# A routed mixer loop: x is added before the routing work of VectorE, the choice is cut in two, the router's tanh moves by a step

## The chip, the cores and the metric

The kernel runs on one core of a Trainium2 chip. The metric is the device time of one execution in microseconds (us). TensorE multiplies matrices, VectorE, ScalarE and GpSimd work element by element (GpSimd also issues the indirect DMAs), and SyncE issues the plain DMAs. Each engine takes its instructions in program order and waits at semaphores for the others.

## The reference

The kernel computes one layer of a hybrid backbone over 2048 tokens of width 1024. Only the part around the change is shown:

```
x  = x + g1 * mixer(modulate(rmsnorm(x)))      # mixer: LRU half yl, retention half y, times w_out
h2 = modulate(rmsnorm(x))
s  = sigmoid(h2 @ w_router)                    # 64 experts
sb = s + b_router
group score = sum of the two largest sb in each of 8 groups; the best 4 groups stay
eidx  = the 6 largest sb of those groups
gates = s[eidx] / sum(s[eidx]) * 2.5
x  = x + g2 * (routed experts of h2 + shared expert of h2);  out = rmsnorm(x)
```

## The kernel before

The program runs in stages. `front` makes the projections and the LRU. `mixer_out` makes the retention output, the output projection, the residual, the second norm and the routing. `experts` makes the experts, and `final` the last norm. The change is in `mixer_out`, and in the one place of `experts` that routes the last tile.

`mixer_out` is a software pipeline over 16 tiles of 128 tokens (NT = 16). Each engine runs `step(n, par)` for n = -1 to 17, and in step n it works on tiles of different age: `on(n, lag)` guards the work on tile t = n - lag. In program order one step holds:

- **TensorE**: transposes of q for tile n (L1667); the first half of the output products of yl for tile n-1, which waits for the first half of the x of tile n-2 (L1652); transposes of y (L1680); the scores s of tile n, which wait for the tanh of tile n-3 (L1688); `rank` of tile n-4 (L1292); the second half of the yl products and the y products (L1652); transposes of h2 for tile n-2 (L1710); the retention output o of tile n (L1720 to L1722); the router product r of tile n-2 (L1730).
- **VectorE**: qf (L1594), the low part of y (L1598), masked scores (L1601), the low part of yl (L1603); h2 times its norm for tile n-2 (L1609); `place(n-4)`; `choose(n-3)`; the sum x1 of tile n-1 (L1624); y of tile n (L1630).
- **ScalarE**: copy of q (L1539), high part of y (L1543), squares of x1 (L1550), high part of yl (L1554), copies of the transposed h2 (L1560), squares of o (L1567), tanh and sigmoid of the router's product of tile n-2 (L1574, L1576).
- **GpSimd**: qb (L1498) and the retention state (L1500, L1505) of tile n; the norm of tile n-2 (L1512, L1515) and the sum h2 + b2 (L1517); the norm rh of tile n (L1522, L1524); `enlist(n-4)`, which writes the ids (L1313) and issues six indirect DMAs into the experts' lists (L1317).
- **SyncE**: loads of rec, x and yl for tile n+1, of which x and yl wait for the x1 of tile n-1; stores of h2, of its transpose and of x1.

`choose` (L1250) has two halves in one function: 14 counted instructions that find the 6 experts and end in `chosen` (L1277), and then L1278 to L1283, which pick the scores of the 6, sum them, take the reciprocal and write the gates into `entry`. ScalarE's tanh overwrites `th` and then `s`, and so it waits for `entry_done` of the tile before. The router's product and the scores share the PSUM bank `ps_s`.

Of the kernel before, what the change touches and what calls it, by code (L numbers as in the profile page):

```python
# [23 lines left out]
ACT = mybir.ActivationFunctionType  # L24
# [1163 lines left out]
class Routing:  # L1188


    N_TOP = 18

# [57 lines left out]
def choose(dve, R, t, b):  # L1250
# [4 lines left out]
    for g in range(N_GROUPS):  # L1255
# [20 lines left out]
    wait_over_zero(dve, R.rank_done, t)  # L1276
    dve.tensor_reduce(R.chosen[:], R.eq6[:, b].rearrange("p j e -> p e j"), AX.X, ALU.add).then_inc(R.chosen_done, 1)  # L1277
    tops.of(dve.tensor_tensor(R.prod[:], R.eq6[:, b], R.s[:, None, :].broadcast_to(each), ALU.mult))  # L1278
    tops.of(dve.tensor_reduce(R.sel[:], R.prod[:], AX.X, ALU.add))
# [4 lines left out]
                      ALU.mult, ALU.mult).then_inc(R.entry_done, 1)  # L1284
    assert tops.n == R.N_TOP

# [34 lines left out]
def mixer_out(nc, for_dma, io, mod_d, hx_d, rec_d, yl_d, h2_d, h2t_d, sum_d, list_d, sf, ident, R, pre, pre_loaded):  # L1321
# [4 lines left out]
    with ExitStack() as ctx:  # L1326
# [84 lines left out]
        def on(n, lag):  # L1411

            return not isinstance(n, int) or 0 <= n - lag < NT
# [118 lines left out]
        @block.scalar  # L1532
        def _(act):
            def step(n, par):
                if on(n, 0):
                    act.wait_ge(qt_done, n + 1)
                    wait(act, o_done, n)
                    wait(act, qb_done, n)
                    act.activation(q_t[:], ps_q[:], ACT.Copy).then_inc(qt_copied, 1)  # L1539
                if on(n, 1):  # L1540
                    act.wait_ge(yt_done, n)
                    wait(act, u1_done, n - 1)
                    act.activation(y_t[0][:].bitcast(F32R), ps_y[:], ACT.Copy).then_inc(yt_copied, 1)  # L1543
# [18 lines left out]
                if on(n, 0):  # L1562
# [3 lines left out]
                    for h in range(HEADS):  # L1566
                        act.activation(sq_o[:, h], ps_o[:, h * DH:(h + 1) * DH], ACT.Square,  # L1567
                                       accum_out=ms[:, h:h + 1]).then_inc(sqo_done, 1)
                if isinstance(n, int) and n == 2:
                    act.wait_ge(consts_set, 2)  # L1570
                if on(n, 2):
                    act.wait_ge(r_done, n - 1)
                    wait(act, entry_done, n - 2)
                    act.activation(th[:], ps_s[:, 0:N_EXP], ACT.Tanh, scale=0.5).then_inc(th_done, 1)  # L1574
                    act.wait_ge(th_done, n - 1)
                    act.activation(R.s[:], th[:], ACT.Identity, bias=phalf[:], scale=0.5).then_inc(R.s_done, 1)  # L1576
                if isinstance(n, int) and n == 0:
# [6 lines left out]
        def _(dve):  # L1584
# [5 lines left out]
            def step(n, par):  # L1590
# [13 lines left out]
                if on(n, 2):  # L1604
# [5 lines left out]
                                             ALU.mult, ALU.mult).then_inc(h2s_done, 1)  # L1610
                if on(n, 4):
                    place(dve, R, n - 4, par, ps_q)
                if on(n, 3):
                    choose(dve, R, n - 3, 1 - par)
                if on(n, 1):
# [5 lines left out]
                    for i, u_done in enumerate((u0_done, u1_done)):  # L1621
                        c = slice(i * 512, (i + 1) * 512)
                        dve.wait_ge(u_done, t + 1)
                        dve.tensor_tensor(x1[:, b, c], ps_u[:, i], x[:, b, c], ALU.add).then_inc(x1_done, 1)  # L1624
                if on(n, 0):
                    dve.wait_ge(rh_done, n + 1)
                    wait(dve, yt_done, n)
                    for h in range(HEADS):
                        e = slice(h * DH, (h + 1) * DH)
                        last = dve.scalar_tensor_tensor(y[:, e], ps_o[:, e], rh[:, h:h + 1],  # L1630
                                                        rec[:, par, 5 * HD + h * DH:5 * HD + (h + 1) * DH], ALU.mult, ALU.mult)
                    last.then_inc(y_done, 1)
                if isinstance(n, int) and n == NT + 1:
                    place(dve, R, NT - 2, 1 - par, ps_q)
# [183 lines left out]
def experts(nc, for_dma, io, mod_d, h2_d, h2t_d, sum_d, list_d, ident, R, pre, pre_loaded, blocks_row, ends_row):  # L1818
# [12 lines left out]
    with ExitStack() as ctx:  # L1831
# [326 lines left out]
        def _(dve):  # L2158
# [127 lines left out]
            def after(k):  # L2286
                if k == 0:
                    choose(dve, R, NT - 1, 1)
                if k == 1:
                    place(dve, R, NT - 1, 1, ps_r)  # L2290
# [240 lines left out]
```

## Time and profile before

| | |
|---|---|
| time, median of 3 executions | 2761.79 us (2761.6 to 2771.06) |
| the profiled execution | 2760.96 us, span 2759.1 us, mean granted TensorE clock 0.953 |
| TensorE busy | 2517.8 us (91% of the span) |
| VectorE / ScalarE / GpSimd busy | 1749.7 / 1013.7 / 981.2 us |
| HBM traffic | 232 GB/s over the span |

All times of the trace count from the start of the span. The time of the execution is 1.9 us more than the span. Busy is the time in which an engine executed instructions, the waits at semaphores are not in it. The mixer's steps lie between about 840 and 1214 us, so they take an eighth of the span. The granted clock is a share of 2.4 GHz; 0.50 is 1.2 GHz.

### The profile page before, as it was taken

To read this page: it belongs to the slowest core of one execution; us is meant where nothing else is said; L and a number is where in the kernel's file an instruction comes from. 1 tells how busy PE (TensorE), PEld (TensorE's weight loads), DVE (VectorE), ACT (ScalarE), POOL (GpSimd) and SP (SyncE) were. 2 spreads that over 40 slices of the span, in tenths; PEclk is the share of its full clock that TensorE was granted. 3 is DMA by queue.
4 is the path that set the end of the run, shared out by engine and by line. 5 is a ranking of instruction groups with operands and counts; after the bars stand their busy time and mean duration, and the time that the engine had idled before them with its cause. 6 is when DMAs were issued, how large, how long until landed. Compare 5 with 4: busy or idle time off the path is not lost. (4 is left out here: it accounts for less than half of the span.)

```text
span 2759.1 us, 47130 instructions
## 1 busy us (share of the span) xinstructions
PE 2517.8 (91%) x11959; PEld 2032.8 (74%) x11960; DVE 1749.7 (63%) x2738; ACT 1013.7 (37%) x1615; POOL 981.2 (36%) x1008
## 2 busy tenths in 40 slices
PE   7999999999938888949999999999999999999990
PEld 4787777776737777737888888787878878787880
DVE  4663664557315676656547758778785777768683
ACT  2311433342312222221325535455453445535452
POOL 1210025712135565542133333333343333334334
PEclk8999999999969999869999999999999999999995
DMA  7775757664655465435778979889897998979887
GB/s 281 288 278 208 263 205 279 239 236 174 231 201 211 157 160 170 149 107 103 188 216 243 270 200 298 267 235 303 246 303 212 277 274 253 314 192 301 260 243 274
DMA packets 239399, 642.13 MB, mean 233 GB/s; under 512 B 24268, under 2 KB 37904, under 8 KB 223824
## 3 DMA queue, kind: packets, MB, share of 16 engines
q1 hardware_dynamic: 188880, 459.75, 47.4%
q0 software_dynamic: 50432, 181.27, 26.9%
q8 instruction: 48, 0.79, 0.1%
q14 instruction: 39, 0.32, 0.0%
HBM read 463.61 MB, written 177.33 MB: 232 GB/s over the span
## 5 line engine op out<-in xcount | busy, mean ns | idle before, releaser
L2058 POOL DMA_INDIRECT sum_d<-w_shared_raw,give x136 | 237.8, 1748 | 605.1 <-DMA sum_d<-w_shared_raw,give 300.8
L2343 PE MATMUL ps_h<-w_exp_hi,x_exp_t_hi 128*128 (+1 forms) x1216 | 311.9, 399 | 23.1 <-ACT w_exp_hi L2099 21.5
L2343 PE MATMUL ps_h<-w_exp_hi,x_exp_t_lo 128*128 (+1 forms) x1216 | 321.9, 407 | 0.0
L2163 DVE TENSOR_TENSOR w_exp_lo<-w_exp,w_exp_hi (+1 forms) x256 | 307.4, 1222 | 8.9 <-ACT w_exp_hi L2099 3.9
L2343 PE MATMUL ps_h<-w_exp_lo,x_exp_t_hi 128*128 (+1 forms) x1216 | 309.8, 397 | 0.0
L2125 ACT ACTIVATE h_exp_t_hi<-ps_ht 128x256 fp32r<-128x256 f32 x152 | 58.6, 385 | 634.6 <-PE ps_ht L2352 626.2
L2343 PEld LDWEIGHTS ps_h<-w_exp_hi,x_exp_t_hi 128*128 128x128 f32 x1216 | 229.4, 189 | 79.2 <-ACT w_exp_hi L2099 21.7
L1134 PE MATMUL ps_p<-wa_hi,hx_split 128*128 128x512 f32 x1088 | 279.1, 402 | 5.3 <-DVE kvqg_out L100 3.3
L2343 PEld LDWEIGHTS ps_h<-w_exp_lo,x_exp_t_hi 128*128 128x128 f32 x1216 | 229.0, 188 | 55.9
L2099 ACT ACTIVATE w_exp_hi<-w_exp (+1 forms) x256 | 255.6, 1056 | 28.8 <-DMA w_exp<-in_experts 25.8
L2343 PEld LDWEIGHTS ps_h<-w_exp_hi,x_exp_t_lo 128*128 128x128 f32 x1216 | 217.7, 189 | 41.4
L1134 PEld LDWEIGHTS ps_p<-wa_hi,hx_split 128*128 128x128 f32 x1088 | 205.5, 190 | 52.3 <-DVE kvqg_out L100 4.0
L2205 DVE SCALAR_TENSOR_TENSOR w_shared_raw<-ps_y,gate,g_row 128x512 f32<-128x512 f32 x272 | 191.5, 746 | 77.3 <-PE ps_y L2343 56.4
L2343 PE MATMUL ps_y<-w_exp_hi,h_exp_t_hi 128*128 (+1 forms) x608 | 204.2, 417 | 17.0 <-DVE h_exp_t_lo L2183 15.7
L2343 PE MATMUL ps_y<-w_exp_lo,h_exp_t_hi 128*128 (+1 forms) x608 | 192.8, 399 | 0.0
L2343 PE MATMUL ps_y<-w_exp_hi,h_exp_t_lo 128*128 (+1 forms) x608 | 192.6, 398 | 0.0
L2048 POOL DMA_INDIRECT w_shared_raw<-h_d,take x139 | 150.4, 1082 | 108.7 <-POOL take L2046 100.5
L2177 DVE TENSOR_TENSOR x_exp_t_lo<-ps_x,x_exp_t_hi 128x512 fp32r<-128x512 f32 x274 | 175.6, 683 | 0.0
L2221 DVE SCALAR_TENSOR_TENSOR h_gated<-tanh_e,ps_h 128x256 f32<-128x256 f32 x152 | 64.0, 421 | 165.9 <-ACT tanh_e L2130 159.6
L2183 DVE TENSOR_TENSOR h_exp_t_lo<-ps_ht,h_exp_t_hi 128x256 fp32r<-128x256 f32 x152 | 64.4, 423 | 155.9 <-ACT h_exp_t_hi L2125 145.7
L2168 DVE TENSOR_TENSOR w_exp_lo<-w_exp,w_exp_hi (+1 forms) x130 | 153.0, 1219 | 0.1
L2119 ACT ACTIVATE x_exp_t_hi<-ps_x 128x512 fp32r<-128x512 f32 x274 | 148.5, 595 | 2.1
(300 smaller groups left out, 4408.0 us busy)
## 6 DMA issues: line engine op xcount, KB each, us to landing
w_exp<-in_experts SPq DMA_DIRECT2D x386, 512.0 KB
hx_split<-hx_d SPq DMA_DIRECT2D x54, 1024.0 KB, 5.6
rec_m<-rec_d SPq DMA_DIRECT2D x16, 1536.0 KB, 11.0
hx_d<-hx_split SPq DMA_DIRECT2D x18, 1024.0 KB, 5.4
wm_rest<-in_w_mod_rest POOLq DMA_DIRECT2D x16, 1024.0 KB, 5.9
rec_d<-kvqg_out SPq DMA_DIRECT2D x48, 256.0 KB, 4.3
xt<-in_xt POOLq DMA_DIRECT2D x18, 512.0 KB, 8.4
rec_d<-kt_kvf_out SPq DMA_DIRECT2D x32, 256.0 KB, 4.3
```

The source lines that it names most:

```text
L1134: last = pe.matmul(ps_p[:, s % 2], hx0[:, at, x, k].bitcast(F32R), wa[w][:, k, p % 2 * HD:(p % 2 + 1) * HD].bitcast(F32R), start=(m + k == ...
L2048: pool.indirect_dma_start(xg[:, par], None, h2_d[:, :], bass.IndirectOffsetOnAxis(take[:, par:par + 1], 0)).then_inc(gathered[par], 16)
L2058: pool.indirect_dma_start(sum_d[:, :], bass.IndirectOffsetOnAxis(give[:, par:par + 1], 0), y[:, par], None, compute_op=ALU.add).then_inc(a ...
L2099: act.activation(w[0][:, piece(e, i)].bitcast(F32R), raw(e, i), ACT.Copy).then_inc(gu_hi, 1)
L2119: act.activation(x_t[0][:, par, b * 512:(b + 1) * 512].bitcast(F32R), ps_x[:, b], ACT.Copy).then_inc(xt_hi, 1)
L2163: dve.tensor_tensor(w[1][:, piece(e, i)].bitcast(F32R), raw(e, i), w[0][:, piece(e, i)], ALU.subtract).then_inc(gu_lo, 1)
L2168: dve.tensor_tensor(w[1][:, piece(e, i)].bitcast(F32R), raw(e, i), w[0][:, piece(e, i)], ALU.subtract).then_inc(wd_lo, 1)
L2177: dve.tensor_tensor(x_t[1][:, par, c].bitcast(F32R), src, x_t[0][:, par, c], ALU.subtract).then_inc(xt_lo, 1)
L2183: dve.tensor_tensor(h_t[1][:, par].bitcast(F32R), ps_t[:, 0:D_EXP], h_t[0][:, par], ALU.subtract).then_inc(ht_lo, 1)
L2205: dve.scalar_tensor_tensor(y[:, par, c], ps_y[:, i], gate[:, bass.ds(k, 1)], g2[:, c], ALU.mult, ALU.mult).then_inc(y_done, 1)
L2221: own.of(dve.scalar_tensor_tensor(hg[:, par], th[:, par], 1.0, ps_h[:, par, 0:D_EXP], ALU.add, ALU.mult))
L2343: last = pe.matmul(out, x[:, j * P:(j + 1) * P].bitcast(F32R), w_part[:, bass.ds(w_at + j * stride, 512)].bitcast(F32R), start=(start and ...
```

## The change

In VectorE's step the sum x1 of tile n-1 now stands ahead of `place` and `choose`. `choose` ends with `chosen`, and the rest of it is a function `gates`, which stands behind the scaling of y. On ScalarE the tanh and the sigmoid of a tile move from the end of one step to the next step, behind the copy of q. In `experts` the two functions follow each other as before.

```diff
 class Routing:
-    N_TOP = 18
+    N_TOP, N_CHOICE = 18, 14
@@ choose
     dve.tensor_reduce(R.chosen[:], R.eq6[:, b].rearrange("p j e -> p e j"), AX.X, ALU.add).then_inc(R.chosen_done, 1)
+    assert tops.n == R.N_CHOICE
+
+def gates(dve, R, t, b):
+    tops = Count(dve, R.top_own, t * R.N_TOP + R.N_CHOICE)
+    each = [P, TOP_K, N_EXP]
     tops.of(dve.tensor_tensor(R.prod[:], R.eq6[:, b], R.s[:, None, :].broadcast_to(each), ALU.mult))
     tops.of(dve.tensor_reduce(R.sel[:], R.prod[:], AX.X, ALU.add))
     tops.of(dve.tensor_reduce(R.ssum[:], R.sel[:], AX.X, ALU.add))
...
     dve.tensor_scalar(R.entry[:, b, :, 1].bitcast(F32), R.sel[:], R.ssum[:], ROUTE_SCALE,
                       ALU.mult, ALU.mult).then_inc(R.entry_done, 1)
@@ mixer_out, scalar
+            def scores(t):
+                act.wait_ge(r_done, t + 1)
+                wait(act, entry_done, t)
+                act.activation(th[:], ps_s[:, 0:N_EXP], ACT.Tanh, scale=0.5).then_inc(th_done, 1)
+                if t == 0:
+                    act.wait_ge(consts_set, 2)
+                act.wait_ge(th_done, t + 1)
+                act.activation(R.s[:], th[:], ACT.Identity, bias=phalf[:], scale=0.5).then_inc(R.s_done, 1)
             def step(n, par):
...
                     act.activation(q_t[:], ps_q[:], ACT.Copy).then_inc(qt_copied, 1)
+                if on(n, 3):
+                    scores(n - 3)
...
-                if on(n, 2):
-                    act.wait_ge(r_done, n - 1)
-                    wait(act, entry_done, n - 2)
-                    act.activation(th[:], ps_s[:, 0:N_EXP], ACT.Tanh, scale=0.5).then_inc(th_done, 1)
-                    act.wait_ge(th_done, n - 1)
-                    act.activation(R.s[:], th[:], ACT.Identity, bias=phalf[:], scale=0.5).then_inc(R.s_done, 1)
+                if n == NT + 1:
+                    scores(NT - 1)
@@ mixer_out, vector
-                if on(n, 4):
-                    place(dve, R, n - 4, par, ps_q)
-                if on(n, 3):
-                    choose(dve, R, n - 3, 1 - par)
                 if on(n, 1):
                     t, b = n - 1, 1 - par
...
                         dve.tensor_tensor(x1[:, b, c], ps_u[:, i], x[:, b, c], ALU.add).then_inc(x1_done, 1)
+                if on(n, 4):
+                    place(dve, R, n - 4, par, ps_q)
+                if on(n, 3):
+                    choose(dve, R, n - 3, 1 - par)
                 if on(n, 0):
...
                     last.then_inc(y_done, 1)
+                if on(n, 3):
+                    gates(dve, R, n - 3, 1 - par)
@@ experts, vector
                     choose(dve, R, NT - 1, 1)
+                    gates(dve, R, NT - 1, 1)
```

## Rows read from the trace of the kernel before

**Rows 1.** Timeline of GpSimd, steps 9 and 10: start, us, instruction [idle before].

```profile
1020.14 2.39 POOL L1517 TENSOR_TENSOR h<-h,b_row 128x1024 f32<-128x1024 f32 x1 [1.40 <-DVE h L1609]
...
1027.68 0.45 POOL L1522 TENSOR_SCALAR rh<-ms 128x4 f32<-128x4 f32 x1 [5.16 <-issue]
...
1030.23 1.09 POOL L1317 DMA_INDIRECT list_d<-entry,slot_u  x1 [0.79 <-POOL entry L1313]
...
1036.70 0.96 POOL L1317 DMA_INDIRECT list_d<-entry,slot_u  x1 [0.30 <-issue]
...
1040.06 1.63 POOL L1505 TENSOR_TENSOR sf_m<-sf_decayed,rec_m 128x512 f32<-128x512 f32 x1
...
1044.04 2.39 POOL L1517 TENSOR_TENSOR h<-h,b_row 128x1024 f32<-128x1024 f32 x1 [1.40 <-DVE h L1609]
```

**Rows 2.** Timeline of TensorE, the same steps.

```profile
1007.56 2.04 PE L1652 MATMUL ps_u<-w_out_hi,yl_hi 128*128 128x512 f32 x4 [2.91 <-DVE x L1624]
...
1022.58 1.09 PE L1710 MATMUL ps_tr<-ident,h 128*128 128x128 f32 x8 [0.53 <-POOL h L1517]
...
1026.19 1.90 PE L1730 MATMUL ps_s<-w_router_s,h_t 128*128 128x64 f32 x16
```

**Rows 3.** Timeline of VectorE, the same steps.

```profile
1015.00 1.65 DVE L1603 TENSOR_TENSOR yl_lo<-yl_m,yl_hi 128x512 fp32r<-128x512 f32 x1 [0.73 <-ACT yl_hi L1554]
1018.77 1.28 DVE L1609 SCALAR_TENSOR_TENSOR h<-x,rstd_m,a_row 128x1024 f32<-128x1024 f32 x1 [2.12 <-POOL rstd_m L1515]
...
1020.49 2.45 DVE L1304 TENSOR_TENSOR prod<-eq,slot 128x384 f32<-128x384 f32 x1
...
1028.12 0.81 DVE L1277 TENSOR_REDUCE chosen<-eq 128x64 f32<-128x384 f32 x1
...
1030.61 1.29 DVE L1624 TENSOR_TENSOR x<-ps_u,x_m 128x512 f32<-128x512 f32 x2
```

**Rows 4.** Timeline of ScalarE, the tanh of step 9.

```profile
1030.73 0.23 ACT L1574 ACTIVATE tanh_s<-ps_s 128x64 f32<-128x64 f32 x1 [3.20 <-DVE entry L1283]
```

**Rows 5.** Timeline of GpSimd: the state sum of step 4, L1517 of steps 5 and 15.

```profile
921.01 1.29 POOL L1505 TENSOR_TENSOR sf_m<-sf_decayed,rec_m 128x512 f32<-128x512 f32 x1
...
924.64 2.34 POOL L1517 TENSOR_TENSOR h<-h,b_row 128x1024 f32<-128x1024 f32 x1 [1.40 <-DVE h L1609]
...
1164.69 2.41 POOL L1517 TENSOR_TENSOR h<-h,b_row 128x1024 f32<-128x1024 f32 x1 [1.40 <-DVE h L1609]
```

**Rows 6.** Timeline of TensorE in steps 3 to 5.

```profile
888.57 1.90 PE L1730 MATMUL ps_s<-w_router_s,h_t 128*128 128x64 f32 x16
...
893.98 1.06 PE L1688 MATMUL ps_s<-q_t,rec_m 128*128 128x128 f32 x8
...
903.72 1.04 PE L1710 MATMUL ps_tr<-ident,h 128*128 128x128 f32 x8
...
927.04 1.09 PE L1710 MATMUL ps_tr<-ident,h 128*128 128x128 f32 x8 [3.59 <-POOL h L1517]
```

**Rows 7.** Timeline of VectorE, the scaling of y in step 3.

```profile
891.39 1.13 DVE L1630 SCALAR_TENSOR_TENSOR y_ret<-ps_o,rh,rec_m 128x128 f32<-128x128 f32 x4 [1.75 <-POOL rh L1524]
```

**Rows 8.** Busy time by stretches: us, five engines, granted clock, DMA share, GB/s.

```profile
923.60:927.00 3.40, 0.00 (x0) 0.00 (x0) 3.33 (x4) 0.00 (x0) 2.34 (x1) 1.00 0.00 0
...
1007.00:1010.40 3.40, 2.84 (x7) 2.29 (x8) 2.64 (x7) 0.90 (x3) 2.49 (x4) 0.50 0.69 39
...
1126.60:1133.20 6.60, 5.47 (x14) 4.23 (x15) 3.18 (x9) 1.06 (x3) 5.01 (x6) 0.50 0.48 111
```

**Rows 9.** Timeline of TensorE, the last h2 transposes, step 17.

```profile
1203.61 1.97 PE L1710 MATMUL ps_tr<-ident,h 128*128 128x128 f32 x8 [7.72 <-POOL h L1517]
```

**Rows 10.** Timeline of GpSimd, the norms of steps 16 and 17.

```profile
1183.61 0.19 POOL L1512 TENSOR_SCALAR rstd_m<-ssq_m 128x1 f32<-128x1 f32 x1 [1.38 <-issue]
...
1198.97 0.19 POOL L1512 TENSOR_SCALAR rstd_m<-ssq_m 128x1 f32<-128x1 f32 x1 [1.31 <-issue]
```

**Rows 11.** Timeline of VectorE, its last instruction of the mixer.

```profile
1213.26 0.17 DVE L1307 CAST slot_u<-slot_f 128x6 uint32<-128x6 f32 x1
```

More of the change, by code:

```diff
@@ L1284, in choose @@
                       ALU.mult, ALU.mult).then_inc(R.entry_done, 1)
-    assert tops.n == R.N_TOP
+    assert tops.n == R.N_TOP - R.N_CHOICE
 def rank(pe, R, t, ps):
@@ L1568, in step @@
                                        accum_out=ms[:, h:h + 1]).then_inc(sqo_done, 1)
-                if isinstance(n, int) and n == 2:
-                    act.wait_ge(consts_set, 2)
-                if on(n, 2):
-                    act.wait_ge(r_done, n - 1)
-                    wait(act, entry_done, n - 2)
-                    act.activation(th[:], ps_s[:, 0:N_EXP], ACT.Tanh, scale=0.5).then_inc(th_done, 1)
-                    act.wait_ge(th_done, n - 1)
-                    act.activation(R.s[:], th[:], ACT.Identity, bias=phalf[:], scale=0.5).then_inc(R.s_done, 1)
+                if n == NT + 1:
+                    scores(NT - 1)
                 if isinstance(n, int) and n == 0:
```

## The prediction

> **What bounds the kernel now.** I read the slices of the page first: the change touches only the mixer, about 372 of 2759 us. Then I took one step of it (step 9) from the timelines of the engines, and asked of each engine whether it has idle time and what ends it. The wait that the change takes away is plain: TensorE stands 2.91 us before the first output product until VectorE has added x [rows 2], because the x1 of the tile before is queued behind `place` and `choose` [rows 3]. After that wait the granted clock is 0.50, at 1.2 of 2.4 GHz, for 3.4 us, 2.84 of them busy [rows 8], which costs another 1.4 us.
>
> But a wait that is removed is worth only what no other chain takes back, so the reader should walk around GpSimd. From one L1517 to the next [rows 1, 2]: the sum itself 2.39 us; TensorE starts the h2 transposes 0.05 later, and they and o take 1026.19 - 1022.58 = 3.61; ScalarE's squares bring rh to 1027.68, 1.49; rh and the ids take 2.55 to the first list DMA at 1030.23; the six DMAs end at 1036.70 + 0.96 = 1037.66, 7.43; qb and the two state sums end at 1041.69, 4.03; the norm and VectorE's h2 end at 1044.04, 2.35. The sum is 23.90 us, which is the whole period, with nothing left over. VectorE waits for this chain (2.12 us before L1609 [rows 3]), TensorE waits for it (0.53 us before L1710 [rows 2]), and neither `place`, `choose` nor x1 is a link of it. So GpSimd's round sets the pace. From step 5 to 15 ten periods take 1164.69 - 924.64 = 240.05 us, 24.0 each [rows 5]. The 0.1 above 23.90 comes from later steps in which the clock stays low for 6.6 us [rows 8] and TensorE arrives last.
>
> **x1 earlier.** L1609 ends at 1020.05, by which time the products of the first half are ready, so the two sums (1.29 us [rows 3]) run while GpSimd adds b2 (until 1022.53). Behind them comes `place`, whose L1304 takes 2.45 us in the old place and ends 0.4 us after GpSimd's sum [rows 1, 3]: both read SBUF, and L1304 stands until GpSimd is done. It still ends just after the same moment. So x1 fits into a wait that is there already, and `place` and `choose` end where they did: `chosen` at 1028.93, 6.4 us after L1517's end. I cost x1's move at nothing on VectorE; were that cover gone, it is 1.3 us on an engine that has over 6 us of idle time in the step.
>
> The Trainium skill (GPSIMD Engine Reference, section 8, Key points) says that GpSimd shares its SBUF interfaces with VectorE and that VectorE's instructions with two SBUF inputs contend for them. The 2.45 us agree; x1 has one input in PSUM, and by that page it would not be held up. Held or not, the sum below stays.
>
> **What is late next on TensorE.** The first output product no longer waits. y can start when rh is there: in step 3, 891.39 - 888.57 = 2.82 us after the router product starts, and y ends 1.13 later [rows 6, 7]. Then comes `gates`, which costs 1030.61 - 1028.93 = 1.68 us [rows 3]. Only then may ScalarE's tanh run, 0.12 + 0.23 us [rows 3, 4] plus some 0.1 to be seen. That is 2.82 + 1.13 + 0.2 + 1.68 + 0.4 = 6.2 us after the router product starts, where TensorE reaches the scores after 893.98 - 888.57 = 5.4 [rows 6]. So the divided choice brings a new wait of 0.85 us before L1688, with `rank` and all output products queued behind it. The queue of ScalarE behind the tanh (y's high part, squares of x1, yl's high part) is early enough: all is done before GpSimd leaves its DMAs.
>
> The rest of TensorE's round is 903.72 - 888.57 = 15.15 us from router product to h2 transposes [rows 6]. GpSimd's chain needs 1022.58 + 23.90 - 1026.19 = 20.3 us for the same stretch. The wait goes before L1710: 20.3 - 15.15 - 0.85, less the 0.35 us of the next point, is 3.9 us, with 15 us of dense products ahead of it. All of what is taken from L1652 comes back there, and lies in front of instructions of GpSimd's round.
>
> **What GpSimd gains.** L1505 takes 1.63 us beside VectorE's L1603, which is stretched to 1.65, and 1.29 where they don't meet [rows 1, 3, 5]. With SyncE's loads of x and yl some 7 us earlier and y some 2 us earlier, L1603 is over before GpSimd's DMAs end. Gain 0.35 us a step (bounds 0 and 0.4): the period is 23.55 at full clock, against 24.0: 10 x 0.455 = -4.6 us.
>
> **What the clock takes.** The old long wait stands before output products, outside GpSimd's round, with slack behind it. The new one stands before the h2 transposes and o, 3.61 us inside it. Twelve waits of 2.4 to 3.6 us in the old steps are my sample. After 11 of them the clock was 0.50: six times as in step 9 with 2.7 to 2.84 us busy, five times as in step 13 with about 5.5 us busy [rows 8]; half of that is lost, 1.4 and 2.75 us. After one it stayed at 1.00: the 3.59 us before L1710 in step 5 [rows 6, 8], which is the very place of the new wait. At 0.50 the transposes take 1.97 us instead of 1.04 to 1.09 [rows 2, 9], so these instructions do pay; h2 transposes and o at half clock would take 7.2 us, long enough to hold the whole low stretch. Mean of the twelve: (6 x 1.4 + 5 x 2.75 + 0) / 12 = 1.85 us. Bounds are 0 (as in step 5) and 2.75. I take 1.85, because the wait is longer than any of the twelve. It counts in the ten steps 6 to 15: +18.5 us. In step 5 the wait is only some 2 us, since the new waits of steps 4 and 5 fill it.
>
> The Trainium skill (TensorE: Matmul & The Clock Gate, section Why this matters for your kernels) asks that TensorE be left no long idle gaps between bursts of matmuls, or its clock drops to the lower level. By this rule the new wait costs in every step, and the sum would be the one above or more. The trace agrees in 11 of 12 waits, and disagrees at the one in the place in question.
>
> **Both ends of the loop.** In step 4 GpSimd's DMAs only begin and TensorE has no slack: y of step 3 ends at 891.39 + 1.13 = 892.52, gates and tanh end 2.0 us later, 0.5 to 0.6 after the scores stood at 893.98 [rows 6, 7]: +0.6 us (0 to 1.5). In steps 16 and 17 GpSimd waits 1.38 and 1.31 us for the squares of x1 [rows 10]. There x1 stands behind `choose`, and the change puts it in front, so both go: -2.7 us (0 at least), and VectorE's end of the mixer at 1213.43 [rows 11] moves with them. The loads of the next stage start behind that end, so it counts in full. The work in `experts` is the same instructions in the same order.
>
> **Sum.** -4.6 + 18.5 + 0.6 - 2.7 = +11.8 us on the profiled 2760.96, so 2772.8; the median of the runs is 0.8 above the profiled time, so 2773.6, told as 2774 us. A difference under 0.5% (13.8 us, beyond 2775.6 or below 2748) is what a measurement here can't tell from no change.
>
> **The rivals.**
> *The clock stays up (19%).* The wait before L1710 behaves as in step 5. Then only -4.6 + 0.6 - 2.7 = -6.7 us remain: 2755. For it speaks the only row in the same place, against it eleven others and that the new wait is longer.
> *Every low stretch is the long one (15%).* 10 x 2.75 = 27.5 us: +20.8, 2783, slower than before. It is decided by the mean loss: above (13.8 + 6.7) / 10 = 2.05 us a step the kernel is over 0.5% slower. For it: a longer wait can bring the fall sooner, and so leave more of it to sit through; the last five old waits were all long. Against it: six short ones.
> *TensorE was the bound (6%).* If GpSimd's round could be shortened by what TensorE does earlier, the period would be 23.90 - 2.91 - 1.4 - 0.53 + 0.85 = 19.9, ten times -4.1, so 2721. Against it: GpSimd's round adds up to the period without any gap that x1 ends.
>
> **How the numbers follow.** My forecast (60%) is a mean loss of 1.2 to 2.4 us a step, 2767 to 2779 us; a third of it lies beyond 2775.6. Slower by over 0.5%: 0.20 + 0.15 = 0.35. Faster by over 0.5%: 0.06. Within: 0.59. The range goes from the first rival to the second, 2756 to 2784.
>
> **What would show it.** Right: L1624 starts right behind L1609 and L1652's wait is gone; L1304 near 1.1 us; a wait of about 0.85 us before L1688 ended by the tanh, and one near 3.9 before L1710; clock 0.50 over L1710 and L1720 to L1722; L1505 at 1.29; ten periods of L1517 near 25.4 us each. Wrong: no clock loss in L1710 and o (then the first rival), GpSimd's DMAs or sums of other lengths, or a period below 23.5, which would mean that GpSimd's round is not the bound.

## The result, and the profile after

| | before | after |
|---|---|---|
| median | 2761.69 us (8 executions, 2754.55 to 2771.06) | 2776.61 us (8 executions, 2773.65 to 2778.97) |
| ratio, 95% interval | | 1.0053 (1.0036 to 1.0069) |
| profiled execution, span | 2760.96, 2759.1 us | 2776.44, 2774.5 us |
| VectorE busy | 1749.7 us | 1723.7 us |

The kernel became slower by 14.9 us in the medians, 0.53% by the ratio; forecast were +12.2 us, 0.44%. VectorE is busy for 26 us less, and that bought nothing.

TensorE's timeline of the kernel after, steps 9 and 10, answers to [rows 2]. All line numbers of after stand some way below those of before: h2's sum is L1524 (L1517 before), the h2 transposes L1725 (L1710), the router product L1745 (L1730), the scores L1703 (L1688).

```profile
1007.66 1.90 PE L1745 MATMUL ps_s<-w_router_s,h_t 128*128 128x64 f32 x16
1009.39 0.61 PE L1682 MATMUL ps_qt<-ident,rec_m 128*128 128x128 f32 x4
1009.76 1.17 PE L1667 MATMUL ps_u<-w_out_hi,yl_hi 128*128 128x512 f32 x4
...
1013.78 1.13 PE L1703 MATMUL ps_s<-q_t,rec_m 128*128 128x128 f32 x8 [0.54 <-ACT tanh_s L1545]
...
1022.66 1.09 PE L1667 MATMUL ps_u<-w_out_hi,y_ret_t_lo 128*128 128x512 f32 x4
1027.30 1.97 PE L1725 MATMUL ps_tr<-ident,h 128*128 128x128 f32 x8 [3.55 <-POOL h L1524]
...
1033.75 1.90 PE L1745 MATMUL ps_s<-w_router_s,h_t 128*128 128x64 f32 x16
```

The wait of 2.91 us before the first output product is gone. In its place stand 0.54 us before the scores, ended by the tanh, and 3.55 us before the h2 transposes, ended by GpSimd (0.53 before). The transposes take 1.97 us (1.09 before), and from their start to the router product it is 33.75 - 27.30 = 6.45 us (3.61 before). The windows show the clock there, to be read against [rows 8]:

```profile
core 0: us, PE busy (x) PEld busy (x) DVE busy (x) ACT busy (x) POOL busy (x), PEclk, DMA share, GB/s
927.40:930.80 3.40, 3.40 (x18) 3.40 (x17) 2.82 (x21) 1.19 (x2) 0.00 (x0) 0.51 0.56 231
1002.60:1005.80 3.20, 3.20 (x17) 3.20 (x17) 2.69 (x19) 1.19 (x2) 0.00 (x0) 0.50 0.42 173
1026.60:1033.20 6.60, 5.90 (x28) 5.90 (x29) 5.71 (x27) 1.19 (x2) 0.65 (x1) 0.50 0.57 191
```

The clock stands at 1.2 of 2.4 GHz for 3.4 or for 6.8 us (the windows shown lie just inside), from step 6 on in turn from step to step. In the first kind shown here TensorE is busy through the whole window; in the second the fall comes within the wait, and the window holds 0.7 us of idle time ahead of the transposes.

VectorE, steps 9 and 10, to be read against [rows 3]:

```profile
1023.54 1.28 DVE L1622 SCALAR_TENSOR_TENSOR h<-x,rstd_m,a_row 128x1024 f32<-128x1024 f32 x1 [6.75 <-POOL rstd_m L1522]
1024.74 1.28 DVE L1633 TENSOR_TENSOR x<-ps_u,x_m 128x512 f32<-128x512 f32 x2
...
1026.44 1.22 DVE L1311 TENSOR_TENSOR prod<-eq,slot 128x384 f32<-128x384 f32 x1
...
1032.83 0.81 DVE L1277 TENSOR_REDUCE chosen<-eq 128x64 f32<-128x384 f32 x1
1036.57 1.13 DVE L1643 SCALAR_TENSOR_TENSOR y_ret<-ps_o,rh,rec_m 128x128 f32<-128x128 f32 x4 [2.93 <-POOL rh L1531]
...
1039.17 0.23 DVE L1290 TENSOR_SCALAR entry<-sel,sel_sum 128x6 f32<-128x6 f32 x1
```

x1 stands right behind the scaled h2 and takes 1.28 us, no more than before, though GpSimd's sum runs beside it. `place`'s product takes 1.22 us in place of 2.45. VectorE waits 6.75 us for GpSimd ahead of L1622.

GpSimd, the same steps, to be read against [rows 1]:

```profile
1024.90 2.35 POOL L1524 TENSOR_TENSOR h<-h,b_row 128x1024 f32<-128x1024 f32 x1 [1.40 <-DVE h L1622]
1035.24 0.19 POOL L1529 TENSOR_SCALAR rh<-ms 128x4 f32<-128x4 f32 x1 [8.00 <-issue]
1037.48 1.09 POOL L1324 DMA_INDIRECT list_d<-entry,slot_u  x1 [0.79 <-POOL entry L1320]
...
1044.01 0.96 POOL L1324 DMA_INDIRECT list_d<-entry,slot_u  x1 [0.30 <-issue]
...
1047.37 1.29 POOL L1512 TENSOR_TENSOR sf_m<-sf_decayed,rec_m 128x512 f32<-128x512 f32 x1
...
1050.99 2.35 POOL L1524 TENSOR_TENSOR h<-h,b_row 128x1024 f32<-128x1024 f32 x1 [1.40 <-DVE h L1622]
```

Walk the round again as the prediction did. Sum and handing over 2.40 (2.44 before); transposes and o 6.45 (3.61); to rh 1.49 (1.49); to the first list DMA 2.24 (2.55); the DMAs 1044.97 - 1037.48 = 7.49 (7.43); qb and the state sums to 1048.66, 3.69 (4.03); norm and h2 2.33 (2.35). It is 26.09 us against 23.90: +2.84 for transposes and o in this step with the long low stretch, -0.65 for rh and the state sum. GpSimd's round is still the whole period: each link starts right behind the one before it, as before.

Where the 15.4 us between the two spans lie, from the starts of h2's sum in both traces:

| stretch | before | after | difference | forecast |
|---|---|---|---|---|
| start of the span to the sum of step 2, all of it work that the change does not touch | 861.82 | 857.57 | -4.25 | 0 |
| steps 2 to 5 (the loop fills) | 62.82 | 67.08 | +4.26 | +0.6 |
| steps 5 to 15, ten periods | 240.05 | 253.60 | +13.55 | +12.05 |
| step 15 to the experts' first instruction | 58.80 | 58.24 | -0.56 | -0.85 |
| experts to the end | 1535.61 | 1538.01 | +2.40 | 0 |

The prediction counts the clock in steps 6 to 15 and leaves step 5 out. The transposes of step 15 lie behind the ten periods, so nine of its ten losses of 1.85 us belong to the third row (-4.6 + 16.65 = +12.05) and the tenth to the fourth (-2.7 + 1.85 = -0.85).

The first and the last row are no work of the change: in the profiles of the twelve experiments below the first lies anywhere from 851.1 to 859.6 and the last from 1532 to 1542. So a single profile carries some us of chance there. The ten periods don't: kernels that came out alike in them lie 0.9 us apart (before and e7) or 1.3 us (after, e1, e2 and e11), and they are the sharp measure in what follows.

### The profile page after: what moved, and what is told of

Same layout as the page of the kernel before. It is cut to its first block and busy times, and to the rows that moved or that the text cites. A ratio compares the mean times of both kernels' runs of the same rounds, so it can differ in the third digit from the quotient of the medians.

```text
span 2774.5 us, 47130 instructions
## 1 busy us (share of the span) xinstructions
PE 2524.0 (91%) x11959; PEld 2042.0 (74%) x11960; DVE 1723.7 (62%) x2738; ACT 1012.5 (36%) x1615; POOL 979.4 (35%) x1008
## 5 line engine op out<-in xcount | busy, mean ns | idle before, releaser
L2140 ACT ACTIVATE h_exp_t_hi<-ps_ht 128x256 fp32r<-128x256 f32 x152 | 58.4, 384 | 635.2 <-PE ps_ht L2368 635.2
```

## The experiments

The medians of before beside these kernels were 2760.2 (e1 to e4), 2759.8 (e5 to e8) and 2762.3 us (e9 to e12), and the ratios go by them. "Ten periods" is steps 5 to 15 as above.

| kernel | median, us | ratio to before, 95% | ten periods |
|---|---|---|---|
| before / after | 2761.7 / 2776.6 | 1.0053 | 240.05 / 253.60 |
| e1, x1 first alone | 2772.41 | 1.0052 (1.0036 to 1.0069) | 252.84 |
| e2, choice divided and tanh late alone | 2777.31 | 1.006 (1.0043 to 1.0077) | 253.05 |
| e3, after with TensorE kept busy | 2758.16 | 0.999 (0.9977 to 1.0003) | 236.09 |
| e7, before with TensorE kept busy | 2762.03 | 0.9998 (0.9983 to 1.0014) | 240.90 |
| e4, before with 1.3 us more on GpSimd | 2797.25 | 1.0131 (1.0115 to 1.0148) | 271.03 |
| e8, e4 with TensorE kept busy | 2770.75 (one) | | 256.93 |
| e11, after with two buffers of scores | 2773.43 | 1.0034 (1.002 to 1.0047) | 252.30 |
| e6, before with its list DMAs cut in two | 2726.02 | 0.9871 (0.9847 to 0.9896) | 213.71 |
| e5, after with the same | 2747.0 | 0.9946 (0.9925 to 0.9967) | 225.13 |
| e10, e5 with x1 behind `place` | 2723.92 | 0.9861 (0.9831 to 0.989) | 207.07 |
| e12, e6 with x1 behind `place` | 2725.01 | 0.9866 (0.9841 to 0.9891) | 207.14 |
| e9, e10 with two buffers of scores | 2729.33 | 0.987 (0.9846 to 0.9894) | 216.71 |

### The two halves of the change

**e1_x_first_only** is before with one edit, x1's block ahead of `place` and `choose`:

```diff
+                if on(n, 1):
+                    t, b = n - 1, 1 - par
...
                 if on(n, 4):
                     place(dve, R, n - 4, par, ps_q)
                 if on(n, 3):
                     choose(dve, R, n - 3, 1 - par)
-                if on(n, 1):
-                    t, b = n - 1, 1 - par
...
```

> The kernel before with only the x1 sum moved ahead of place and choose; the choice stays whole and the tanh at the end of its step. My theory (GpSimd's round sets the pace, TensorE's idle time moves in front of the h2 transposes, and the clock falls there): the long wait before the h2 transposes is there as in the changed kernel, 3.5 to 4.1 us, the clock is 0.50 over h2 transposes and o, ten periods of GpSimd's h2 sum (steps 5 to 15) near 253 us, and the time 2770 to 2777. The squares of x1 are not behind the tanh here, so GpSimd's waits in steps 16 and 17 go (about 2 us off the changed kernel). Rival (it is the division of the choice and the later tanh that cost, by the wait before the scores): the ten periods stay at 240 us or fall, time 2745 to 2762.

As expected in time and periods. The waits before the transposes are longer than the 3.5 to 4.1 us expected, and GpSimd's wait in step 17 stayed, to which the account of the end of the mixer comes back. Measured +12.2 us and ten periods of 252.84. This one move alone brings 12.8 of the 13.55 us that the steps lose. TensorE's timeline of e1, the h2 transposes of steps 9 and 10:

```profile
1024.24 1.97 PE L1710 MATMUL ps_tr<-ident,h 128*128 128x128 f32 x8 [4.20 <-POOL h L1517]
...
1049.42 1.97 PE L1710 MATMUL ps_tr<-ident,h 128*128 128x128 f32 x8 [4.95 <-POOL h L1517]
```

**e2_split_only** is after with x1 put back behind `place` and `choose`; the divided choice and the late tanh stay.

> The changed kernel with x1 back behind place and choose: only the divided choice and the later tanh. My theory: x1 ends 1.7 us earlier than before, so the wait before the first output product is near 1.2 us and about 0.5 us stand before the scores; the rest of TensorE's idle time, about 3 us, stands before the h2 transposes, where the clock falls in some steps or in all. Ten periods between 236 and 250 us, time 2757 to 2773. Rival (the divided choice costs by itself): ten periods at 252 us or more although the wait before the h2 transposes is short.

This missed. It is as slow as the whole change (253.05), with the same wait of 3.5 us at the same place and none before the output products. So either half of the change is enough by itself, and the two don't add. TensorE's timeline of e2:

```profile
1013.80 1.13 PE L1703 MATMUL ps_s<-q_t,rec_m 128*128 128x128 f32 x8 [0.54 <-ACT tanh_s L1545]
...
1027.31 1.65 PE L1725 MATMUL ps_tr<-ident,h 128*128 128x128 f32 x8 [3.53 <-POOL h L1524]
```

The reason, as far as the waits tell it: in before x1 is done 2.91 us after TensorE comes for it. Without `gates` ahead of it (five instructions, 1.7 us) x1 is done 1.7 us earlier; and once transposes and o run at half clock, TensorE comes about 2 us later in the round. Together that is over 2.91, so TensorE finds x1 done, goes through to the transposes, waits there, and loses its clock there again. By this the same program order can hold its wait in either place, and each state keeps itself up. I had reckoned with the first of the two terms only. This is worked out from the waits; no run tests it alone, but e4 below goes over in the same way, and e8, which is e4 with the clock held up, goes back.

### Does the low clock make the loss, and does its place matter

**e3_fill** is after with 14 products of constants behind the output products of steps 5 to 15; what they write is overwritten and used by nothing.

```diff
+                if 5 <= n <= 15:
+                    wait(pe, ht_copied, (n - 3) * 2 + 1)
+                    for _ in range(14):
+                        pe.matmul(ps_t[:, 0], wo[0][:, 0, 0:P].bitcast(F32R), wo[0][:, 0, 0:512].bitcast(F32R),
+                                  start=True, stop=True)
                 if on(n, 2):
                     pe.wait_ge(h2_done, n - 1)
```

> The changed kernel with 14 products of 128x512 on constant operands in steps 5 to 15, between the output products and the h2 transposes; their result is overwritten and used by nobody. They take 14 x 0.233 = 3.3 us of the 3.55 us in which TensorE stands there. My theory (the clock is what the change costs): the granted clock is 1.00 over h2 transposes and o, GpSimd's period is 23.5, ten periods 235 us instead of 253.6, and the time falls by 18 to 20 us below the changed kernel, to 2756 to 2760, slightly below the kernel before. Rival (the period is longer for another reason, such as the later tanh or GpSimd's own work): more work for TensorE gains nothing, the ten periods stay at 253 or grow.

As expected. The granted clock is 1.00 through all ten periods; transposes and o take 25.39 - 21.78 = 3.61 us as before, and the period is 23.57 (42.90 - 19.33). TensorE's timeline of e3:

```profile
1021.78 1.09 PE L1730 MATMUL ps_tr<-ident,h 128*128 128x128 f32 x8 [0.39 <-POOL h L1524]
...
1025.39 1.90 PE L1750 MATMUL ps_s<-w_router_s,h_t 128*128 128x64 f32 x16
```

GpSimd's, of the same kernel:

```profile
1019.33 2.40 POOL L1524 TENSOR_TENSOR h<-h,b_row 128x1024 f32<-128x1024 f32 x1 [1.40 <-DVE h L1622]
...
1042.90 2.41 POOL L1524 TENSOR_TENSOR h<-h,b_row 128x1024 f32<-128x1024 f32 x1 [1.40 <-DVE h L1622]
```

Useless work makes the kernel 18 us faster (2776.6 to 2758.2), and the ten periods fall by 17.5. So all of the loss in the ten periods hangs on the low clock; the 23.6 us left are the prediction's base period of 23.55.

**e7_fill_before** is before with 12 such products where TensorE waits for x1, ahead of the first output product.

> The kernel before with 12 products of 128x512 on constant operands (2.8 us, result overwritten and unused) in the 2.9 us in which TensorE waits for x1, steps 5 to 15. My theory: the low clock behind this wait costs 1.4 us or more of TensorE's time, but lies outside GpSimd's round. With the clock at 1.00 the period stays 23.9 in every step; only the 0.1 us a step of the late long low stretches go. Ten periods 239 to 240, time 2758 to 2762. Rival (a low stretch costs wherever it stands): ten periods 15 to 20 us shorter.

The clock is 1.00 in nine of the ten steps, and it is worth nothing: 240.90 against 240.05. TensorE now waits 1.75 us at the transposes instead of 0.53, as its timeline of e7 shows (steps 7, 9 and 10):

```profile
969.72 1.49 PE L1715 MATMUL ps_tr<-ident,h 128*128 128x128 f32 x8 [1.93 <-POOL h L1517]
...
1018.72 1.09 PE L1715 MATMUL ps_tr<-ident,h 128*128 128x128 f32 x8 [1.74 <-POOL h L1517]
...
1042.56 1.09 PE L1715 MATMUL ps_tr<-ident,h 128*128 128x128 f32 x8 [1.75 <-POOL h L1517]
```

In step 7 the clock fell over the transposes, for 3.4 us behind a wait of 1.93 us, and this period alone is 25.13 us, where its neighbours are 24.04 and 23.85. So a low stretch of 3.4 us is free over the output products, and over the transposes and o it costs: 1.1 to 1.3 us in this step of e7, 2.08 us in the mean of after's short and long ones. The prediction put the 0.1 us by which before's periods exceed 23.90 down to its long low stretches. That isn't shown, as e7's nine periods without a fall are 23.97 us in the mean, and so its 240.90 lie above the 239 to 240 expected.

**e4_gpsimd_plus** is before with one product of 128x512 more on GpSimd in each step from step 5 on; nothing uses its result.

```diff
...
                     pool.tensor_tensor(qb_t[:], q_t[:], xi[:, 1], ALU.mult).then_inc(qb_done, 1)
+                    if n >= 5:
+                        wait(pool, spare_done, n - 5)
+                        pool.tensor_tensor(spare[:], xi[:, 0], xi[:, 1], ALU.mult).then_inc(spare_done, 1)
```

> The kernel before with one more GpSimd product of 128x512 (about 1.3 us, result unused) behind qb in steps 5 to 15. My theory (GpSimd's round is the whole period): the ten periods grow by the length of the added instruction each, 13 us or somewhat less where VectorE's contention changes, and the waits of TensorE grow; with a longer wait before the h2 transposes the clock may add to it. Time 2772 to 2785. Rival (the wait for x1 sets the pace, GpSimd has room): ten periods stay within 2 us of 240.

The direction was right and the size missed: +31 us over ten periods, of which the product itself (1.30 us each) is 13. TensorE's timeline of e4:

```profile
1033.30 1.97 PE L1715 MATMUL ps_tr<-ident,h 128*128 128x128 f32 x8 [5.22 <-POOL h L1522]
1039.53 1.90 PE L1735 MATMUL ps_s<-w_router_s,h_t 128*128 128x64 f32 x16
1042.18 1.16 PE L1657 MATMUL ps_u<-w_out_hi,yl_hi 128*128 128x512 f32 x4 [0.31 <-DVE x L1629]
```

Here too the wait has moved from x1 (0.31 left of 2.91) to the transposes, 39.53 - 33.30 = 6.23 us at the low clock. **e8_gpsimd_plus_fill** adds 7 of e3's products to it, in the same place as there.

> The kernel with one more GpSimd product in steps 5 to 15 and, besides, 7 products of TensorE (1.6 us) in front of the h2 transposes in the same steps. If the 31 us that the ten periods grew by were 12.5 us of GpSimd and 18 us of clock, then here the clock over h2 transposes and o is 1.00 and the ten periods take about 252 us. If they stay near 270 us, the added instruction costs more than its own time.

Ten periods of 256.93: 14.1 us come back, 5 us fewer than the expected 252 would give. The first two steps still lose their clock over the transposes and o, with periods of 26.3 and 26.4. From step 7 on it is up there, and TensorE's wait stands before x1 again, as in before. TensorE's timeline of e8:

```profile
1011.01 2.05 PE L1657 MATMUL ps_u<-w_out_hi,yl_hi 128*128 128x512 f32 x4 [2.90 <-DVE x L1629]
```

The periods are then 25.1 to 25.4 us, 1.2 to 1.5 above before's 23.9, which is little more than the added product. The three of 26.1 follow a low stretch of 6.8 us over the output products, after which TensorE comes to the transposes without a wait, 1.1 us late in step 9. Where TensorE isn't late, GpSimd's round sets the pace nearly one for one.

### The tanh's wait

**e11_two_scores_only** is after with two buffers of the router's scores, so that the tanh of step t waits for the gates of t - 1:

```diff
-        self.s = sb("s_r", [P, N_EXP])
+        self.s = sb("s_r", [P, 2, N_EXP])
...
-                wait(act, entry_done, t)
+                wait(act, R.chosen_done, t)
+                wait(act, entry_done, t - 1)
...
```

> The changed kernel with two buffers for the scores and nothing else changed: the tanh waits for the choice of the tile before, not for its gates. The wait of 0.54 us before the scores goes, and the wait before the h2 transposes grows by as much, to about 4.1 us, since GpSimd's round sets the pace. So ten periods stay at 250 to 256 us; only the start of the loop (67.1 us from the first to the fourth h2 sum) gets shorter by some 2 to 4 us. Time 2770 to 2776. Rival (the tanh's wait is what costs in each step): ten periods 248 or less.

As expected: no wait before the scores, 4.12 us before the transposes instead of 3.55, ten periods of 252.30. In a full step the tanh's wait costs next to nothing. Where the loop fills, steps 2 to 5 take 64.93 us in place of 67.08, but in these steps after had a fall of its clock that e11 hadn't. e3, which is the same program as after up to step 5 and had no such fall either, takes 65.51; so 0.6 us of the 2.15 are the tanh's wait and 1.6 the fall.

### Shortening the round that sets the pace

GpSimd stands idle from its sum of h2 until rh (5.16 us in before [rows 1], 8.00 in after), and then issues six list DMAs of 1.27 us, which the rest of the round stands behind. **e6_lists_split_before** issues three of them in that idle time and three behind rh (`enlist` gets a range for it; the ids are written ahead of the first three):

```diff
                     pool.tensor_tensor(h2[:, par], h2[:, par], b2[:], ALU.add).then_inc(h2_done, 1)
+                if on(n, 4):
+                    enlist(pool, R, n - 4, par, list_d, range(3))
...
                 if on(n, 4):
-                    enlist(pool, R, n - 4, par, list_d)
+                    enlist(pool, R, n - 4, par, list_d, range(3, TOP_K))
```

**e5_lists_split_after** is the same edit of after.

> The kernel before with the same cut of the list DMAs. GpSimd's round is as short as in the changed kernel with the cut, but x1 stands behind place, choose and gates, so TensorE waits some 3 us for it before the first output product, and the clock falls there with nothing behind it that hides the loss: VectorE's h2 sum, place, choose and x1 (about 8.9 us after the h2 sum of GpSimd) and then 14 us of TensorE make 22 to 23 us, with the clock's loss 23 to 24. Ten periods 225 to 240 us, time 2745 to 2762. If the early x1 is worth nothing even then (rival), this kernel is as fast as the changed kernel with the cut, within 5 us.

> The changed kernel with GpSimd's six list DMAs cut in two: the ids and three DMAs go out between the h2 sum and rh, where GpSimd stands idle for 5 us or more, the other three behind rh. If GpSimd's round is the bound, it gets shorter by three DMAs of 1.27 us, less some 0.7 us that rh comes later: about 20.5 us at full clock; TensorE's own work is 15.15 + 3.6 us and about 1.3 us of waiting for the tanh, 20.1 us. So hardly any wait stays before the h2 transposes, the clock stays at 1.00, and ten periods take 200 to 210 us instead of 253.6. Time 2718 to 2735. Rival (the later tanh or VectorE takes over as the bound): ten periods above 225 us.

Both gain, and both expectations missed, as the time of each kernel came out where the other's was expected. Before gains 35.7 us, after 29.6 and ends 21 us behind. With the round of GpSimd shorter, TensorE comes to the h2 transposes last in both, without a wait, and there the old place of x1 is the better one. In e5 VectorE, standing at x1 ahead of `place`, waits for TensorE's last products (VectorE's timeline of e5):

```profile
1013.24 0.69 DVE L1640 TENSOR_TENSOR x<-ps_u,x_m 128x512 f32<-128x512 f32 x1 [0.58 <-PE ps_u L1674]
...
1015.94 0.69 DVE L1640 TENSOR_TENSOR x<-ps_u,x_m 128x512 f32<-128x512 f32 x1 [2.01 <-PE ps_u L1674]
```

Behind that, `place` is late, with it the first list DMA, rh and y, and it comes back to TensorE as 0.93 us before y's transposes and 1.46 before the scores. GpSimd's timeline of e5:

```profile
1019.17 1.07 POOL L1329 DMA_INDIRECT list_d<-entry,slot_u  x1 [3.88 <-DVE slot_u L1314]
```

And TensorE's:

```profile
1003.82 0.66 PE L1702 MATMUL ps_yt<-ident,y_ret 128*128 128x128 f32 x4 [0.93 <-DVE y_ret L1650]
1005.93 1.13 PE L1710 MATMUL ps_s<-q_t,rec_m 128*128 128x128 f32 x8 [1.46 <-ACT tanh_s L1552]
```

In e6 no wait for TensorE stands ahead of `place`; TensorE's own wait for x1 comes in every second step or so, 2.3 to 2.9 us, and the periods are 20.4 to 21.9. That the late `place` is what holds e5 back is read from these rows; the next kernel tests it.

**e10_x_behind_place** is e5 with x1 between `place` and `choose`, to have `place` early and x1 not behind the choice:

```diff
-                if on(n, 1):
-                    t, b = n - 1, 1 - par
...
                 if on(n, 4):
                     place(dve, R, n - 4, par, ps_q)
+                if on(n, 1):
+                    t, b = n - 1, 1 - par
...
                 if on(n, 3):
                     choose(dve, R, n - 3, 1 - par)
```

> The changed kernel with the list DMAs cut in two and x1 between place and choose; one buffer of scores, so the tanh still waits for the gates. The wait before the transposes of y (0.92 us with x1 ahead of place) goes to about 0, the one before the scores (1.46) to about 0.9. Ten periods 197 to 212 us against 225.1 with x1 ahead of place, time 2720 to 2735. Rival (x1's place does not matter): ten periods at 222 or more.

As expected: ten periods of 207.07, all 20.7, against e5's 225.13, under 0.1 us of waiting before y's transposes and none before those of h2, and the clock up through all ten. The wait before the scores was 1.46 us where I expected 0.9. TensorE comes last at the transposes now, so this wait should cost, and I tried to take it away.

**e9_two_scores** is e10 with the two buffers of e11.

> The changed kernel with the list DMAs cut in two (three before rh), with x1 between place and choose, and with two buffers for the scores s, so that the tanh waits only for the choice of the tile before and not for its gates. What I learned from the kernels with the cut: once TensorE sets the pace, x1 ahead of place waits for TensorE's last output product and holds back place, GpSimd's lists, rh and y, and the gates behind y hold back the tanh and the scores. Both are gone here. TensorE's own work is 18.8 us a step, GpSimd's round about 19.1. Ten periods 190 to 200 us, time 2708 to 2722. Rival (the two waits are only pushed elsewhere): ten periods above 210, no faster than the kernel before with the cut.

Missed, and the rival that it names came out: the wait is only pushed elsewhere. The wait before the scores is gone and every second step is down to 19.2 us, but the others take 22.5 to 25.2, behind a new wait at `rank`. TensorE's timeline of e9:

```profile
1020.42 0.63 PE L1299 MATMUL ps_qt<-chosen,order_s 128*128 128x64 f32 x4 [3.37 <-issue]
```

VectorE's, ahead of that:

```profile
1016.93 2.80 DVE L1290 TENSOR_SCALAR entry<-sel,sel_sum 128x6 f32<-128x6 f32 x1
```

GpSimd's, beside it:

```profile
1017.41 1.29 POOL L1510 TENSOR_TENSOR qb_t<-q_t,xi_s 128x512 f32<-128x512 f32 x1
1018.63 1.06 POOL L1512 TENSOR_TENSOR sf_decayed<-sf_m,gc_m 128x512 f32<-128x512 f32 x1
```

The last instruction of `gates`, six numbers a row and 0.23 us elsewhere, takes 2.80 us and ends at 1019.73, with the second of these two sums of GpSimd (1019.69). qf is queued behind it on VectorE, and TensorE needs what qf read out of PSUM before it writes there again. That qf is what `rank` waits for is read from the order of the program; the row itself names no releaser.

**e12_x_behind_place_whole** is e6 with x1 between `place` and `choose`, the choice whole and the tanh in its old place.

> The kernel before with the list DMAs cut in two and x1 between place and choose; the choice is whole, the tanh at the end of its step. x1 is early without the two new waits of the change. The choice with its gates ends near 7.7 us after the h2 transposes start, y near 8.8, where TensorE wants it at 8.6. Ten periods 190 to 205 us against 213.7 with x1 in the old place, time 2708 to 2722. Rival (an early x1 gains nothing even here): ten periods at 213 or more.

A narrow miss at 2725.0. The ten periods fall from e6's 213.71 to 207.14 (19.5 and 22.0 in turn), but the start of the loop takes 60.97 in place of 58.40 and its end 58.4 in place of 56.5; a wait for y of 1.75 and 0.6 us in turn is what is left on TensorE. The profile of e6 is of its fastest execution, 8 us under its median, and up to step 2 it is 7.1 us shorter than that of e12; so the spans of these two profiles can't be compared. e6, e10 and e12 can't be told apart in the median. Each is 1.3 to 1.4% faster than before, and further ahead of after.

## Why the prediction was right

**GpSimd's round sets the pace: right.** The round adds up to the period in both traces, e4 and e8 lengthen it and the period goes with it, e6 shortens it and 36 us are gained. The rival in which TensorE was the bound is out: in e1 TensorE no longer waits 2.91 us for x1 and nothing is faster. (Its 2721 us left out the forecast's own terms for both ends, -2.1 us; nothing hangs on it.)

**x1 costs nothing on VectorE: right**, by the cover that was named; 1.28 us in a wait. L1311 took 1.22 us (forecast 1.1).

**The new waits: right in place, off in size.** Before the scores 0.54 us (forecast 0.85), before the transposes 3.55 (3.9). e11 shows that the first matters to nobody in a full step.

**The clock: right in mechanism, 1.85 us forecast, 2.08 measured.** From transposes to router product the steps 5 to 14 take 5.67 us in the mean, against 3.59 before. The low stretches were short in six of these steps and long in four, much as the sample of twelve had it (six short, five long, one without a fall); but nearly all of each lies over instructions that pay, and the 3.59 us wait that had stayed at full clock in step 5 found no follower. Step 5, which the prediction left out because its wait would be some 2 us, waited 2.68 us, lost its clock too and paid 5.25 - 3.61 = 1.64 us. e3 is the proof, since it changes nothing but TensorE's idle time. The Trainium skill advises to leave TensorE no long idle gaps between bursts (TensorE: Matmul & The Clock Gate, Why this matters for your kernels). The trace of after agrees in these ten steps, with waits of 2.68 to 4.01 us and a fall at each; what a fall costs is another matter: in e7 before's falls were gone in nine of ten steps, and that gained nothing.

**GpSimd's gain: 0.455 us forecast, 0.7 measured.** 25.36 - 2.08 is a base period of 23.3. The state sum gave its 0.34; the other 0.3 is the rh instruction (0.45 to 0.19 us) and h2's sum (2.39 to 2.35), which no longer meet VectorE's work. That second part comes only with the low clock: in e3 rh takes 0.45 us and h2's sum 2.40 again, and the period is 23.6, the forecast's own.

For the ten periods the forecast was +12.05 us. Step 5 adds 1.6 to it, the larger loss in the other nine steps 2.5, and the larger gain takes 2.6 off, which makes the 13.55 measured. That the last two hide each other is luck.

**The start of the loop: the term that was mis-sized, +0.6 forecast, +4.3 measured.** VectorE's timeline of the kernel after, where step 3 is followed by step 4:

```profile
878.28 0.69 DVE L1633 TENSOR_TENSOR x<-ps_u,x_m 128x512 f32<-128x512 f32 x1 [2.51 <-PE ps_u L1667]
880.99 0.69 DVE L1633 TENSOR_TENSOR x<-ps_u,x_m 128x512 f32<-128x512 f32 x1 [2.02 <-PE ps_u L1667]
...
887.56 1.13 DVE L1643 SCALAR_TENSOR_TENSOR y_ret<-ps_o,rh,rec_m 128x128 f32<-128x128 f32 x4 [0.31 <-POOL rh L1531]
...
890.22 1.25 DVE L1290 TENSOR_SCALAR entry<-sel,sel_sum 128x6 f32<-128x6 f32 x1
```

TensorE's, from there to step 5:

```profile
891.94 1.13 PE L1703 MATMUL ps_s<-q_t,rec_m 128*128 128x128 f32 x8 [2.03 <-ACT tanh_s L1545]
...
893.27 2.01 PE L1667 MATMUL ps_u<-w_out_hi,yl_hi 128*128 128x512 f32 x4
...
914.41 1.13 PE L1703 MATMUL ps_s<-q_t,rec_m 128*128 128x128 f32 x8 [1.46 <-ACT tanh_s L1545]
```

Without list DMAs h2 comes early in these steps, and x1, now first in VectorE's queue, waits for products that TensorE hasn't made. That pushes `choose` right up to y, which then starts 0.3 to 0.4 us late, and the last instruction of `gates` is stretched by 1.0 us. The tanh is late by both, and the scores wait 2.03 us where 0.6 was forecast; from the h2 sum of step 3 to that of step 4 it is 20.91 us in place of 18.80. Then the clock falls over the output products (2.01 us for four, 1.17 elsewhere), in a step that has no slack. e3, the same program up to step 5, waits as long and kept its clock there, as TensorE's timeline of e3 shows:

```profile
893.90 1.13 PE L1703 MATMUL ps_s<-q_t,rec_m 128*128 128x128 f32 x8 [2.03 <-ACT tanh_s L1545]
...
895.23 1.18 PE L1667 MATMUL ps_u<-w_out_hi,yl_hi 128*128 128x512 f32 x4
```

Its steps 2 to 5 take 65.51 us. So of the 4.26 us of these profiles 1.6 are this fall, which can come or stay away in the same steps of the same program, 2.1 are the longer step 3, and at most 0.6 is left for the wait of 1.46 us in step 5. e1, with x1's move alone, shows +1.0.

**The end of the mixer: -0.85 forecast, -0.56 measured, from larger errors.** The forecast took both waits of GpSimd's norm away, 2.7 us. In step 16 the wait of 1.38 us did go; in step 17 it only went from 1.31 to 1.03 us. x1 was early there, but the squares of it did not follow. ScalarE of the kernel after, in step 17:

```profile
1210.18 0.23 ACT L1545 ACTIVATE tanh_s<-ps_s 128x64 f32<-128x64 f32 x1 [6.94 <-DVE entry L1290]
...
1210.69 1.04 ACT L1569 ACTIVATE sq_out_x<-x 128x1024 f32<-128x1024 f32 x1
```

They are queued behind the tanh, which waits 6.94 us for the gates. Rows 10 name no releaser for GpSimd's waits, so that they are for the squares was read from the order of the program. e11 bears it out: its tanh doesn't wait for these gates, and the wait of the norm is down to 0.07 us. e1 does too, against its expectation: with the tanh in its old place the squares still stand behind it, it waits 6.94 us there as well, and 1.02 us of the norm's wait stay. The prediction asked what is queued behind the tanh for the full steps, where GpSimd's DMAs cover it, and did not ask it again for the last step, where nothing does.

That is 1.0 us less than forecast. It is nearly made up for: the low clock of step 15 took 4.95 - 3.55 = 1.40 us where 1.85 was forecast, and TensorE, 0.4 us late for step 15's transposes in before, is on time in after.

**The whole.** Forecast +11.8 us on the profiled execution, measured +15.4: 3.7 more at the start of the loop, 1.5 in the ten periods, 0.3 at the end, and 1.9 less from the two ends of the profile, by chance.

**What stays open.** Why the wait of 3.59 us in step 5 of before kept its clock and 2.68 us in step 5 of after did not, nor 1.93 us in step 7 of e7, where the other nine waits of 1.7 to 2.1 us at this place did; why e12, with 6.6 us less in its ten periods than e6, loses 4.5 of them again at the two ends of the loop; and the -4.25 and +2.4 us at both ends of the profile, put down to chance only because kernels that share that work spread as wide.

## What to carry to other kernels

A wait of TensorE that you take away comes back further on in its round, as long as another engine sets the pace; ask where, and whether the instructions behind the new place lie inside the round that sets the pace, because they are the ones that may run at the low clock. Work through the first and the last steps of a pipelined loop by themselves: slack that covers a queue in a full step is missing there, and here the first steps alone held 3.7 us of error in a sum of 12. If a round is the bound, look for its longest waits and put its own work into them: three DMAs issued from an earlier place were worth more than twice what all of this change cost.

## What the runs showed of the hardware that I had not expected

- A `TENSOR_SCALAR` of 128x6 on VectorE, with one SBUF tensor read, took 2.80 us (e9) and 1.25 us (after) beside GpSimd's work on SBUF, against 0.23. Small size is no protection. Both ended with an instruction of GpSimd, at 1019.73 and 1019.69 us in e9 and at 891.47 and 891.45 in after, which looks like a wait for its end. x1, with one input in PSUM and 512 columns, took 0.69 us a piece beside GpSimd's sum, as always.
- The falls of the clock in the ten periods of the kernel after lasted 3.4 or 6.8 us, from step 6 on in turn from step to step, behind waits of which most were the same 3.55 us.
- A list DMA holds GpSimd's queue for 1.27 us, 0.96 busy and 0.30 to the next, six of them for 7.5 us, 29% of the step: more than any sum in it.
